# Two decoder layers on one core: the convolution's last steps ahead of the attention gating, and a wait for three blocks of four

## The reference, cut to what matters

```
z = h @ w_in                      # q, k, v | u (2048) | gates (2048)
o = attention(q, k, v)            # three dilated groups merged -> (256, 256)
y_attn = o @ attn_wo              # (256, 256) @ (256, 1024)
hc = a * sigmoid(g)               # a, g = halves of u
hc = depthwise causal conv, 31 taps, over tokens, + bias
y_conv = silu(layer_norm(hc)) @ conv_wo
y = sigmoid(g_attn) * y_attn + sigmoid(g_conv) * y_conv
x = x + gate * (y @ w_out)
```

## Time and profile before

| | |
|---|---|
| median of 3 runs | 1281.35 us (1281.32 to 1281.73) |
| the profiled execution's own time | 1281.08 us |
| its span in the profile | 1279.3 us |
| TensorE busy | 1234.3 us, 96% |
| VectorE busy | 965.5 us, 75% |
| ScalarE busy | 546.9 us, 43% |
| DMA | 293.44 MB, 229 GB/s in the mean |
| mean granted TensorE clock | 0.995 |

### The profile page before, as it was taken

One profiled execution on the slowest core, in us unless ns is written; L12 is line 12 of the kernel. 1 busy time (PEld: TensorE's weight loads), 2 busy tenths in 40 slices (PEclk: granted clock), 3 DMA queues, 4 the chain that ended last, 5 costly groups with the idle time before them and its releaser, 6 DMA issues.

```text
span 1279.3 us, 13844 instructions
## 1 busy us (share of the span) xinstructions
PE 1234.3 (96%) x5440; PEld 957.3 (75%) x5448; DVE 965.5 (75%) x1341; ACT 546.9 (43%) x576; POOL 2.2 (0%) x5
## 2 busy tenths in 40 slices
PE   3999999999999999999999999999999999999997
PEld 2588887766776887888878888876676678888885
DVE  5698886699997576988668888668999866644443
ACT  3343434532344555344355433354323564634431
POOL 0000000000000000000000000000000000000000
PEclk9999999999999999999999999999999999999999
DMA  9989994444233539889747889545532335455540
GB/s 375 416 317 373 375 377 177 184 179 166 100 113 118 191 111 377 345 342 356 301 170 276 343 344 356 193 162 204 188 133 99 132 132 196 167 197 189 193 177 34
DMA packets 52913, 293.44 MB, mean 229 GB/s; under 512 B 6640, under 2 KB 6896, under 8 KB 27120
## 3 DMA queue, kind: packets, MB, share of 16 engines
q1 hardware_dynamic: 51120, 289.38, 60.4%
q10 hardware_dynamic: 1728, 3.17, 0.7%
HBM read 291.45 MB, written 1.07 MB: 229 GB/s over the span
## 4 chain that ended last, share of the span: by engine, by line
PE 90%; DVE 3%; DMA 3%; ACT 2%; issue 1%; SPq 0%; DVEq 0%
PE ps L329 24%; PE ps L331 24%; PE ps L330 24%; PE ps L348 12%; DMA raw<-in_weights 2%; PE ps L515 1%; PE ps L396 1%; PE ps L537 1%; DMA ada_raw<-in_ada_w 1%; DVE hF L1084 1%; PE ps L526 0%; PE ps L485 0%; ACT L715 0%; DVE w_lo L997 0%; PE ps L380 0%
## 5 line engine op out<-in xcount | busy, mean ns | idle before, releaser
L997 DVE TENSOR_TENSOR w_lo<-raw,w_hi 128x2048 fp32r<-128x2048 f32 x176 | 401.0, 2286 | 40.8 <-ACT w_hi L709 40.5
L709 ACT CAST w_hi<-raw 128x2048 fp32r<-128x2048 f32 x176 | 334.5, 1910 | 163.7 <-PE ps L331 82.9
L329 PE MATMUL ps<-w_hi,hA_hi 128*128 128x512 f32 (+1 forms) x992 | 397.7, 401 | 2.9 <-DVE hA_lo L997 2.9
L331 PE MATMUL ps<-w_hi,hA_lo 128*128 128x512 f32 (+1 forms) x992 | 385.2, 388 | 0.0
L330 PE MATMUL ps<-w_lo,hA_hi 128*128 128x512 f32 (+1 forms) x992 | 384.6, 388 | 0.0
L329 PEld LDWEIGHTS ps<-w_hi,hA_hi 128*128 128x128 f32 x992 | 187.4, 189 | 46.6 <-issue 11.9
L330 PEld LDWEIGHTS ps<-w_lo,hA_hi 128*128 128x128 f32 x992 | 187.7, 189 | 38.5 <-issue 3.3
L331 PEld LDWEIGHTS ps<-w_hi,hA_lo 128*128 128x128 f32 x992 | 187.2, 189 | 38.9
L1186 DVE SCALAR_TENSOR_TENSOR work<-conv_in,par,work 128x256 f32<-128x256 f32 x480 | 193.7, 478 | 0.0
L1012 DVE SCALAR_TENSOR_TENSOR product<-ada_raw,c_bc 128x1024 f32<-128x1024 f32 x144 | 171.6, 1220 | 15.6 <-DMA ada_raw<-in_ada_w 15.2
L348 PE MATMUL ps<-raw,hF 128*128 128x512 f32 x384 | 171.6, 598 | 5.5 <-ACT hF L734 5.5
(11 more groups left out here) (120 smaller groups left out, 741.8 us busy)
## 6 DMA issues: line engine op xcount, KB each, us to landing
raw<-in_weights SPq DMA_DIRECT2D x200, 1024.0 KB, 4.8
ada_raw<-in_ada_w SPq DMA_DIRECT2D x144, 512.0 KB, 6.7
gate_bc<-gate_scratch ACTq DMA_DIRECT2D x6, 512.0 KB, 6.3
x<-in_x_tok SPq DMA_DIRECT2D x1, 1024.0 KB, 7.4
out_tok<-xn_h SPq DMA_DIRECT2D x4, 256.0 KB, 2.2
c_bc<-in_c_row SPq DMA_DIRECT2D x1, 512.0 KB, 4.4
c_bc<-in_g_row SPq DMA_DIRECT2D x1, 512.0 KB, 5.6
mask_all<-in_mask SPq DMA_DIRECT2D x1, 416.0 KB, 16.3
```

Source lines behind the costliest of these rows:

```text
L329: nc.tensor.matmul(out_ap, stat[0], mov[0], start=start, stop=False)
L331: return nc.tensor.matmul(out_ap, stat[1], mov[0], start=False, stop=stop)
L709: nc.scalar.copy(w_hi[:, s % HI, :], raw[:, p % RAW, :]).then_inc(hi_done, 1)
L997: return nc.vector.tensor_tensor(dst, whole, hi_part.bitcast(F32), ALU.subtract)
```

## The change

On VectorE the last 4 steps of the convolution are issued ahead of the gating of the attention output, not behind it. Within the gating the halves of each tile swap: half 1, then half 0. On TensorE the wait ahead of panel 24 asks for three gated blocks of the layer, not four; the wait for the fourth now stands ahead of `conv_out`. With the new order the first three blocks are both of tile 0, and half 1 of tile 1: the banks 2, 0 and 3. No instruction is added but the second wait, which is taken along by the next instruction.

```diff
                 conv_turn(2)
                 conv_turn(3)
-                pe.wait_ge(ya_done, 4 * (l + 1))
+                pe.wait_ge(ya_done, 4 * l + 3)
                 def ln_turn(hf):
...
+                pe.wait_ge(ya_done, 4 * (l + 1))
                 conv_out(0, (0, 1))
                 pe.wait_ge(g3_done, l + 1)
...
                 conv(10)
                 conv_stats(0)
+                conv(steps)
                 dve.wait_ge(sig_gate_done, 3 * l + 1)
                 for tt in range(TT):
                     if tt == 0:
                         dve.wait_ge(ao_done, l + 1)
                     else:
                         dve.wait_ge(panel_done, base + M_AO + 1)
-                    for half in range(2):
+                    for half in (1, 0):
                         c = slice(half * 512, half * 512 + 512)
                         nc.vector.tensor_tensor(y[:, tt, c], acc(half, tt), gates[:, tt, c], ALU.mult).then_inc(ya_done, 1)
-                conv(steps)
                 conv_stats(1)
```

## The result

| | before | after |
|---|---|---|
| median of 6 runs each | 1280.92 us (1279.91 to 1281.73) | 1272.49 us (1272.15 to 1273.35) |
| span in the profile | 1279.3 us | 1270.5 us |
| TensorE busy | 1234.3 us, 96% | 1230.7 us, 97% |

The ratio of the runs is 0.9936, with a 95% interval of 0.9923 to 0.9949. The forecast was 1273.0 us. The kernel before was run again beside the changed one, and so its median is 1280.92 us here and not 1281.35.

A forecast was written before the change was run, and what follows sets the result against it. TensorE bounds the kernel, through its work, waits and slow matmuls. Gains of 4.16 and 4.18 us in the two layers, 8.34 off 1281.08, give 1272.74; with 0.27 for the median, 1273.0 us, range 1271.9 to 1275.5.

The forecast's parts named there:

- The place and the mechanism: At conv_turn(3) TensorE waits 2.52 us for four steps behind VectorE's gating; moved ahead, they end before TensorE needs them.
- The stretch: TensorE from the start of conv_turn(2) to that of ln_turn(0): 6.53 us, from 10.69 and 10.71 in the two layers.
- The wait for the third block: TensorE ahead of panel 24 waits for gated half 1 of tile 1: 0.2 us, bounds 0 and 0.3.
- The cover on VectorE: VectorE's idle time around tile 0's gating, 1.59 us, just holds the four moved steps, 1.58 us.
- The layer norm in time: Scaling half ready at 401.75, TensorE at ln_turn(0) at 403.10: no wait, 1.35 us left.
- The split between wait and clock: Of each layer's gain, some 2.3 us are the wait at conv_turn(3), some 1.85 panel 24's matmuls at 1.2 GHz.
- both falls of the clock: Behind the wait at conv_turn(3), in both layers, the granted clock drops to 0.53 and panel 24's matmuls take 0.4275 us.
- The clock did not fall behind the eight transposes: Rivals on panel 24's clock: it falls anyway, 1276.7 us, chance 0.06; it stays down longer, 1286.1 us, chance 0.04.
- ScalarE did not come late: Rival: panel 28's late copy delays the square root, TensorE waits 0.6 us more at ln_turn(0) per layer; 1274.2 us, chance 0.07.
- nothing else held `conv_turn(3)`: Rival: something else holds conv_turn(3) or panel 24 for as long; time stays at 1281.4 us, chance 0.03.
- the weights' loads hold TensorE up nowhere: Claim on the whole kernel: TensorE's list of waits names no DMA, so weight loads cost it 0 us.
- The "eight matmuls" of panel 25: Between ln_turn(0) and ln_turn(1): eight matmuls taking 3.44 us, so ln_turn(1) comes 4.31 us behind and does not wait.

The follow-up runs named there:

- the steps alone: Against the kernel before: four convolution steps moved ahead of the gating, halves in old order, TensorE waiting for all four blocks; 1274.1 us, ratio 0.9951.
- the swap alone: Against the kernel before: halves swapped and TensorE waiting for three blocks, the four steps still behind the gating; 1280.29 us, ratio 1.0001.
- The filled gap: Against the kernel before: 22 needless transposes put between conv_turn(2) and conv_turn(3), where TensorE stood still; 1277.75 us, ratio 0.9979.

## Why the prediction was right

- **The place and the mechanism.** The wait at `conv_turn(3)` was the work of four steps behind four blocks of gating, and it went when they were swapped. Shown by the steps alone, and by the number of steps left behind the gating: with two the stretch is 8.3 us, with four 10.7 (9.07 once, where the clock stayed up), with eight 12.3 and 13.4.
- **The stretch.** Forecast 6.53 us, measured 6.52 and 6.53; forecast gain 8.34 us, measured 8.35 in the two stretches. The medians differ by 1280.92 - 1272.49 = 8.43. That the time came out 0.5 us under the forecast is for the most part the 0.43 us by which the kernel before was faster when it was run again.
- **The wait for the third block.** I took 0.2 us out of 0 to 0.3; it was 0.19, of which 0.17 went when the signal came earlier. That the old order of the halves, with its wait for the fourth block, would cost 0.6 more is shown, at 0.60.
- **The cover on VectorE.** I called it just as large as the work. It was 0.2 us larger. The prediction's own times have tile 0's gating end at 396.66 and tile 1's start at 396.77: that is 0.1 us, and the overlap of these two neighbours' ends is the other 0.1.
- **The layer norm in time.** The sums, the square root and the scaling came within 0.1 us of the forecast starts once the changed trace's own 0.11 us is taken off, and TensorE waited for none of it.
- **The split between wait and clock.** I gave the wait some 2.3 us of a layer and the clock 1.85. With the wait and no fall the stretch is 9.07, so the wait is worth 9.07 - 6.52 = 2.55 and the fall 10.70 - 9.07 = 1.63. The sum was right and its parts were each off by 0.2: the price of starting again behind a wait I had put on the clock.
- **What I had taken for certain.** I took both falls of the clock as given, since both stood in the one profile. The kernel before has since shown them in 8 of 8 layers, but the run with the swap alone shows that they can stay out at the same wait. If they stay out in one layer of ten, the gain is 2 x 1.63 x 0.1 = 0.3 us less on average; this is an estimate from ten layers. The filled gap put the clock's share at 2.7 us and not at 3.3, with an interval of 1.4 to 3.8 that holds both.
- **The rivals.** The clock did not fall behind the eight transposes (1.00 in both layers), ScalarE did not come late, nothing else held `conv_turn(3)`, and TensorE's pace in panel 24 was full from its first matmul on.
- **What the prediction read wrongly.** It says that the weights' loads hold TensorE up nowhere, since its list of waits names no DMA. The list names only the last engine ahead of TensorE. At 504.03 TensorE waits 0.87 us for `mid_lo`, behind a copy of ScalarE that had stood idle for 8.43 us until its panel landed, and the page's chain has 2% of `DMA raw<-in_weights`. So waits that hang on loads exist, and they could have taken a part of the gain back or given more. They moved by 0.4 us in all. That it would be so little wasn't worked out ahead, and here it was luck that it came out small. The "eight matmuls" of panel 25 are also four float32 matmuls of two records each; the 3.44 us stand.

The changed kernel without the swap but with the wait for three blocks was not tried: with the old order the third block is half 0 of tile 1, and panel 24 would write over the unread half 1.

## What to carry to other kernels

A wait of TensorE costs more than its length where it is long enough for the clock to fall: here a wait of 2.5 us had a price of 4.2 (10.69 - 6.52), a wait of 1.7 one of 1.8 (8.32 - 6.52). So look for the first matmuls behind a wait, not only at the wait, and it can be worth it to cut a wait in part. When work is moved ahead on an engine, add up the idle times between its other pieces there; if they hold it, the move is free, and what comes over them came through in full here. Order the pieces behind a shared release by which of them the bounding engine needs first.

## What the runs showed of the hardware

- The fall of the granted clock depends on more than the wait's length: behind the same 2.52 us it came 9 times out of 10, and once, in layer 1 of the kernel with the swap alone, it didn't. Behind 0.50 to 1.73 us it came in none of 6. It can come when TensorE has already been at work again for almost 1 us.
- Float32 transposes held the clock up as matmuls did: 22 of them in the gap of 2.5 us, and it stayed at 1.00 in both layers, as with 11 matmuls.
- A float32 matmul of 128x256 took 0.43 us at 2.4 GHz, as two records of 0.216; a float32 transpose of 128x128 is one record, 0.109 us from start to start.
